# Weight splits placed behind the next copies, the first loads reordered, and one-column PSUM clears in a four-block transformer kernel

## The reference

```python
for l in range(2):                                   # first block
    h = h + 0.5 * swiglu(rmsnorm(h, g[l, 0]), ffn weights[l, 0])      # 1024 -> 2816 -> 1024
    u = rmsnorm(h, g[l, 1])
    cols = u @ w_in[l]                               # queries, keys, values of four attentions
    y_a, y_b, y_c, y_d = mla(..), window(..), nsa(..), diff(..)       # 512 channels each
    merged = sum(sigmoid(u @ w_gate[l, b]) * (y_b @ w_branch[l, b]))
    h = h + merged @ w_o[l]
    h = h + 0.5 * swiglu(rmsnorm(h, g[l, 2]), ffn weights[l, 1])
x = rmsnorm(h, final_g)
for i in range(2):                                   # second block
    x = x + 0.5 * rms_norm(swiglu(rms_norm(x, g[0])), g[1])
    m = dilated_attention(rms_norm(x, g[2])) if i == 0 else retention(rms_norm(x, g[2]))
    x = x + rms_norm(m, g[3])
    x = x + 0.5 * rms_norm(swiglu(rms_norm(x, g[4])), g[5])
```

## Time and profile before

| | |
|---|---|
| median of 3 runs | 2826.56 us (2824.9 to 2827.1) |
| profiled execution | 2825.75 us, span 2823.9 us |
| TensorE matmuls busy | 2744.4 us, 97% |
| VectorE, ScalarE busy | 1879.5 us (67%), 1387.9 us (49%) |
| chain that ended last | TensorE 86%, VectorE 7%, ScalarE 3% |
| DMA | 488.46 MB, 173 GB/s on average |

### The profile page before, as it was taken

One profiled execution on the slowest core, in us unless ns is written; L12 is line 12 of the kernel. 1 busy time (PEld: TensorE's weight loads), 2 busy tenths in 40 slices (PEclk: granted clock), 3 DMA queues, 4 the chain that ended last, 5 costly groups with the idle time before them and its releaser, 6 DMA issues.

```text
span 2823.9 us, 42094 instructions
## 1 busy us (share of the span) xinstructions
PE 2744.4 (97%) x16902; PEld 2401.5 (85%) x16902; DVE 1879.5 (67%) x2830; ACT 1387.9 (49%) x1950; POOL 104.0 (4%) x135
## 2 busy tenths in 40 slices
PE   7999999999999999999999999998999998999998
PEld 6888999788888989988878889997888888988787
DVE  5666678666776657867677666555667766755666
ACT  4554455454545445545555544444545454453544
POOL 1000000000000000001011001110000000000000
PEclk9999999999999999999999999999999999999999
DMA  6454443445445543346545545543554554434443
GB/s 245 180 197 164 152 157 135 179 160 197 173 184 187 193 168 147 135 162 229 183 179 195 186 175 172 175 154 136 196 181 167 188 183 155 176 134 172 164 178 127
DMA packets 49046, 488.46 MB, mean 173 GB/s; under 512 B 6480, under 2 KB 6576, under 8 KB 10520
## 3 DMA queue, kind: packets, MB, share of 16 engines
q1 hardware_dynamic: 43192, 470.44, 45.2%
q0 software_dynamic: 5728, 16.25, 2.1%
HBM read 485.47 MB, written 1.19 MB: 172 GB/s over the span
## 4 chain that ended last, share of the span: by engine, by line
PE 86%; DVE 7%; ACT 3%; issue 1%; DMA 1%; POOL 0%; DVEq 0%; ACTq 0%; SPq 0%; POOLq 0%
PE ps L859 67%; PE ps L919 15%; DVE ring_lo L1861 2%; ACT ring_hi L1504 1%; PE ps L875 1%; PE ps L1133 1%; DMA norm_g<-norm_gT_dram 1%; PE ps L1341 1%; DVE ring_lo L1874 1%; PE ps L1356 1%; DVE xn L1990 0%; ACT ring_hi L1555 0%; PE ps L1248 0%; DVE ring_lo L1917 0%; DMA ring<-stream_dram 0%
## 5 line engine op out<-in xcount | busy, mean ns | idle before, releaser
L859 PE MATMUL ps<-uT,ring_hi 128*128 128x512 f32 (+1 forms) x5536 | 1510.1, 344 | 9.8 <-DVE qkT L2020 8.3
L859 PE MATMUL ps<-uT,ring_lo 128*128 128x256 f32 x4176 | 1176.1, 282 | 0.0
L859 PEld LDWEIGHTS ps<-uT,ring_hi 128*128 128x128 f32 x5536 | 954.7, 190 | 144.5 <-issue 8.8
L859 PEld LDWEIGHTS ps<-uT,ring_lo 128*128 128x128 f32 x4176 | 794.4, 190 | 6.2
L1954 DVE TENSOR_TENSOR ring_lo<-ring,ring_hi 128x2048 fp32r<-128x2048 f32 x160 | 366.8, 2292 | 221.2 <-ACT ring_hi L1555 221.2
L1861 DVE TENSOR_TENSOR ring_lo<-ring,ring_hi 128x3072 fp32r<-128x3072 f32 (+1 forms) x114 | 365.3, 3205 | 181.7 <-ACT ring_hi L1504 181.4
L1504 ACT ACTIVATE ring_hi<-ring 128x3072 fp32r<-128x3072 f32 (+1 forms) x114 | 301.8, 2648 | 244.9 <-PE ps L859 224.5
L1555 ACT ACTIVATE ring_hi<-ring 128x2048 fp32r<-128x2048 f32 x167 | 317.4, 1901 | 0.0
L919 PE MATMUL ps<-ring_hi,hid_hi 128*128 128x512 f32 x704 | 276.7, 393 | 0.0
L919 PE MATMUL ps<-ring_lo,hid_hi 128*128 128x512 f32 x704 | 276.0, 392 | 0.0
L919 PE MATMUL ps<-ring_hi,hid_lo 128*128 128x512 f32 x704 | 274.0, 389 | 0.0
(11 more groups left out here) (314 smaller groups left out, 2778.1 us busy)
## 6 DMA issues: line engine op xcount, KB each, us to landing
ring<-stream_dram SPq DMA_DIRECT2D x299, 1536.0 KB, 6.3
mlaT_all<-bias_vectors POOLq DMA_DIRECT2D x32, 96.0 KB, 2.9
bias<-gains_dram POOLq DMA_DIRECT2D x5, 512.0 KB, 7.8
yR<-bias_vectors POOLq DMA_DIRECT2D x1, 2048.0 KB, 10.8
mlaT_all<-bias_vectors POOLq DMA_DIRECT2D x32, 64.0 KB, 2.9
row<-ret_const_dram POOLq DMA_DIRECT2D x1, 1280.0 KB, 5.7
h<-x_rows_dram POOLq DMA_DIRECT2D x2, 512.0 KB, 11.6
yR<-gains_dram POOLq DMA_DIRECT2D x2, 512.0 KB, 10.7
```

What stands on the lines that cost most here:

```text
L859: m = pe.matmul(out_, lhsT, rhs, start=start, stop=stop, **kw)
```

## The change

1. **Start.** SyncE issues table and picks, h, constants and gains, then slot 0's gate part, slot 0's up part, the first two thirds of slot 1, the last thirds of both, then slots 2 and 3. Slot 0's gate part is split in the middle of the first norm, its up part behind it, slot 1's two thirds behind the squares. GpSimd's parameter loads go behind its first root.
2. **Clears** write one column each.
3. **Mixer, t = 14:** `copy_diff` ahead of the gate, `low_diff` ahead of the gate's scaling.
4. **Output projection of the mixer:** the last third of its first slot is split on its own, early; k = 2 is multiplied first.
5. **Dilated attention:** the low split behind the first eight pieces goes behind the next piece's copy.
6. **Retention:** the query and key tiles lie 3, 3, 3, 3, 2, 2 in their slots, the last two of kind FFN; each low split goes behind the next tile's copy, the first rotation behind tile 7's; a head's last split goes behind the turned copies, and the swish behind the split.

```diff
@@ -72,6 +72,7 @@
 C_RET_QK, C_RET_V, C_RET_O = 6, 16, 6
+QR_FIRST = [0, 3, 6, 9, 12, 14]
@@ -85,12 +86,19 @@
              + _FFN + [WHOLE] * (3 * 8 + C_WO - 1) + [RAW] + _FFN
-             + _FFN + [WHOLE] * (C_RET_QK + C_RET_V + 4) + [RAW] * (C_RET_O - 4) + _FFN)
+             + _FFN + [WHOLE] * (C_RET_QK - 2) + [FFN] * 2 + [WHOLE] * (C_RET_V + 4) + [RAW] * (C_RET_O - 4) + _FFN)
...
+def ret_slot(t):
+    n = max(n for n in range(C_RET_QK) if QR_FIRST[n] <= t)
+    return n, t - QR_FIRST[n]
@@ -330,6 +338,11 @@
         h_in = sem("h_in")
+        gate_0_in = sem("gate_0_in")
+        up_0_in = sem("up_0_in")
+        front_1_in = sem("front_1_in")
+        gate_0_hi = sem("gate_0_hi")
+        gate_0_lo = sem("gate_0_lo")
@@ -745,9 +758,12 @@
         BACK_SLOTS = []
-        for first in [layer_slot(l) + C_FFN for l in range(DEPTH)] + [layer_slot_2(i) + C_FFN for i in range(DEPTH)]:
-            BACK_SLOTS += [first, first + 1]
+        for l in range(DEPTH):
+            BACK_SLOTS += [layer_slot(l) + C_FFN, layer_slot(l) + C_FFN + 1, mix_slot(l) + S_WO]
+        for i in range(DEPTH):
+            BACK_SLOTS += [layer_slot_2(i) + C_FFN, layer_slot_2(i) + C_FFN + 1]
@@ -795,8 +811,8 @@
             if what[0] == "qk":
-                if what[1] % T_PER_SLOT == T_PER_SLOT - 1 or what[1] == QR_T - 1:
-                    split_after(c0 + what[1] // T_PER_SLOT, take, end)
+                if what[1] + 1 in QR_FIRST + [QR_T]:
+                    split_after(c0 + ret_slot(what[1])[0], take, end)
@@ -806,12 +822,21 @@
-            load(stream[0, :, :], 0)
-            sp.wait_ge(table_masked, 1)
...
                 sp.dma_start(picks_sb[0:33, 512 * n:512 * n + 512], pick_1[:, 512 * n:512 * n + 512]).then_inc(picks_in, 16)
-            for s in range(1, NS):
+            loads = [(h[:, 0, :], x_rows[:, 0, :]), (h[:, 1, :], x_rows[:, 1, :]), (cst[:, :], consts),
+                     (norm_g[:, :, :, :], norm_gT)]
+            assert len(loads) == H_DMAS
+            for dst, src in loads:
+                sp.dma_start(dst, src).then_inc(h_in, 16)
+            sp.dma_start(ring[:, 0, 0:D], stream[0, :, 0:D]).then_inc(gate_0_in, 16)
+            sp.dma_start(ring[:, 0, D:2 * D], stream[0, :, D:2 * D]).then_inc(up_0_in, 16)
+            sp.dma_start(ring[:, 1, 0:2 * D], stream[1, :, 0:2 * D]).then_inc(front_1_in, 16)
+            for s in range(2):
+                sp.dma_start(ring[:, s, 2 * D:3 * D], stream[s, :, 2 * D:3 * D]).then_inc(weights_in[s], 16)
+            for s in range(2, NS):
@@ -891,8 +916,13 @@
                 def gate_up(c, t, i=None, first=False, end=False):
-                    split_weights(c, i)
+                    if c:
+                        split_weights(c, i)
                     for part in range(2):
+                        if c == 0 and part == 0:
+                            pe.wait_ge(gate_0_lo, 1)
+                        elif c == 0:
+                            split_weights(c)
@@ -927,7 +957,7 @@
                 for b in range(4):
-                    pe.matmul(ps[:, b, :], zero_bf[:, :], zero_bf[:, 0:1].to_broadcast([1, 512]),
+                    pe.matmul(ps[:, b, 0:1], zero_bf[:, :], zero_bf[:, 0:1],
@@ -956,7 +986,7 @@
                         if ks[0] == 5:
-                            pe.wait_ge(lo_back, 2 * l + a + 1)
+                            pe.wait_ge(lo_back, BACK_SLOTS.index(c) + 1)
@@ -1227,14 +1257,16 @@
                             lambda k: (merged_lo, K_SPLIT * l + k + 1) if k < K_SPLIT
-                            else (merged, 32 * l + branches_before(32) + 1 + k))
+                            else (merged, 32 * l + branches_before(32) + 1 + k), [2, 0, 1] + list(range(3, KD)))
...
                     c = c0 + k // 3
-                    split = SLOT_KIND[c] != RAW
-                    if split:
+                    split, back = SLOT_KIND[c] != RAW, c in BACK_SLOTS and k % 3 == 2
+                    if back:
+                        pe.wait_ge(lo_back, BACK_SLOTS.index(c) + 1)
+                    elif split:
@@ -1248,12 +1280,12 @@
                         elif split:
-                            mm(ps[:, n, :], x_hi[:, k, ts], high(c)[:, cols], k == 0, False)
+                            mm(ps[:, n, :], x_hi[:, k, ts], high(c)[:, cols], k == (2 if c in BACK_SLOTS else 0), False)
...
                             mm(ps[:, n, :], x[:, k, ts], slot(c)[:, cols], False, False)
-                    if k % 3 == 2 or k == nk - 1:
+                    if k % 3 == (1 if c in BACK_SLOTS else 2) or k == nk - 1:
@@ -1293,7 +1325,7 @@
                     if hp == 0 and n in (2, 5):
-                        pe.wait_ge(lo_back, 2 * DEPTH + n // 3 + 1)
+                        pe.wait_ge(lo_back, BACK_SLOTS.index(c) + 1)
@@ -1398,16 +1430,17 @@
-                for t in range(16):
-                    c = c0 + t // 3
+                for t in range(QR_T):
+                    n, place = ret_slot(t)
+                    c = c0 + n
...
                     if t in (2, 5):
-                        pe.wait_ge(lo_back, 2 * DEPTH + 2 + t // 3 + 1)
-                    tile_piece(pc[0], c, t % 3, KD * p if t == 0 else None)
+                        pe.wait_ge(lo_back, BACK_SLOTS.index(c) + 1)
+                    tile_piece(pc[0], c, place, KD * p if t == 0 else None)
...
                     pc[0] += 1
-                    if t % 3 == 2 or t == 15:
+                    if t + 1 in QR_FIRST + [QR_T]:
@@ -1517,8 +1550,17 @@
                     act.activation(dst, src, ACT.Copy, scale=gain[:, k:k + 1]).then_inc(uT_act_ready, 1)
+                    if p == 0 and k == 3:
+                        act.wait_ge(gate_0_in, 16)
+                        act.activation(high(0)[:, 0:D], ring[:, 0, 0:D], ACT.Copy).then_inc(gate_0_hi, 1)
+                if p == 0:
+                    act.wait_ge(up_0_in, 16)
+                    act.activation(high(0)[:, D:2 * D], ring[:, 0, D:2 * D], ACT.Copy).then_inc(hi_ready, 1)
                 act.activation(xn[:, 0, :], h[:, 0, :], ACT.Square, accum_out=h_sq[:, 0:1]).then_inc(h_squared, 1)
+                if p == 0:
+                    act.wait_ge(front_1_in, 16)
+                    act.activation(high(1)[:, 0:2 * D], ring[:, 1, 0:2 * D], ACT.Copy).then_inc(hi_ready, 1)
@@ -1527,6 +1569,8 @@
                     v, c = FT * f + g + 1, c0 + g
+                    if c < 2:
+                        act.wait_ge(weights_in[c], 16)
@@ -1566,6 +1610,12 @@
+            def take_high_unused(c):
+                act.wait_ge(weights_in[c % NS], 16 * (c // NS + 1))
+                act.activation(high(c)[:, 2 * D:], ring[:, c % NS, 2 * D:], ACT.Copy).then_inc(hi_back, 1)
@@ -1637,7 +1687,8 @@
                         copy_2(g, retention_copy)
-                        done_retention(g, take_high)
+                        if what == "qk" or n < 7:
+                            done_retention(g, take_high)
@@ -1664,9 +1715,10 @@
                     copies("row", hh)
-                    swishes(hh)
...
                         copies("turn", hh - 1)
+                    done_retention(ret_piece("row", hh, 7), take_high)
+                    swishes(hh)
@@ -1780,15 +1832,17 @@
                         copy_outputs(l, t - 2)
+                    if t == 14:
+                        copy_diff(l)
...
                         gate(l, merge_at(2 * t))
-                    if t == 14:
-                        copy_diff(l)
...
                 take_high(mix_slot(l) + S_BRANCH_2 + 1)
+                take_high_unused(mix_slot(l) + S_WO)
...
                     if k == 3:
-                        take_high(mix_slot(l) + S_WO)
+                        act.wait_ge(ring_used, emptied_before(mix_slot(l) + S_WO))
+                        take_high_late(mix_slot(l) + S_WO)
@@ -1800,8 +1854,6 @@
-            for c in range(2):
-                take_high(c)
@@ -1884,6 +1936,14 @@
                                              ALU.subtract).then_inc(uT_dve_ready, 1)
+                    if p == 0 and k == 3:
+                        dve.wait_ge(gate_0_hi, 1)
+                        dve.tensor_tensor(ring_lo[:, 0, 0:D], ring[:, 0, 0:D], high(0)[:, 0:D].bitcast(F32),
+                                          ALU.subtract).then_inc(gate_0_lo, 1)
+                if p == 0:
+                    dve.wait_ge(hi_ready, 1)
+                    dve.tensor_tensor(ring_lo[:, 0, D:2 * D], ring[:, 0, D:2 * D], high(0)[:, D:2 * D].bitcast(F32),
+                                      ALU.subtract).then_inc(lo_ready, 1)
@@ -2022,9 +2082,10 @@
                 copy_row(p, 5, True)
+                first_late = []
...
                     copy_2(PIECES_DIL + n, dilated_copy)
-                    done_dilated(n, take_low)
+                    done_dilated(n, take_low if n < 7 else first_late.append)
@@ -2059,6 +2120,8 @@
                     take_pieces(pieces[0:1])
+                    for c in first_late if s == 0 else ():
+                        take_low(c)
@@ -2078,12 +2141,21 @@
```

(52 more changed lines are left out.)

## The result

| | before | after |
|---|---|---|
| median of 4 runs | 2825.73 us | 2790.87 us (2789.35 to 2791.39) |
| profiled execution | 2825.75 us, span 2823.9 | 2790.96 us, span 2789.2 |

The ratio is 0.9881, with a 95% interval of 0.9867 to 0.9894: 1.2% faster, 34.9 us by the medians. Forecast were 2792.0 and a range of 2785 to 2805.

What follows compares the result with a forecast made beforehand. TensorE, its matmuls filling 97% of the span, was taken as the bound, so order should cut its idle time. Terms 8.5+3+2.6+4.3+12.3+3.0 = 33.7 us off 2825.75 gave 2792, range 2785 to 2805.

Steps and rivals of the forecast that it cites:

- The start: First norm and FFN: earlier loads and reordered splits gain 8.5 us, ends 4 and 10.5.
- T: Start: landing of the first norm's loads, put at 8 us; first transposes before the change start at 19.20.
- clears near 19.5: First FFN: sign that the start term holds, with the first norm's transposes near 8.
- The clears: Seven later FFNs: one-column clears save about 0.5 each, less some root waits; 3 us counted, ends 0 and 6.
- up to 2.5 more: Clears: extra gain to the sum if four clears cost 0.1, by the Trainium skill's 25 ns each.
- t = 14, the turns: Mixer step 14, both layers: earlier copies gain 2.6 us; retention's turned heads: copies first gain 3.0 us.
- The output projection: Mixer, both layers: first-slot wait goes, 0.9 returns at the second slot, layer 1's clock stays up; gain 4.3 us.
- Dilated attention and retention's tiles: Copies ahead of splits and new slot layout remove copy waits, a value-slot wait and low clock; gain 12.3 us.
- (a): Rival: new waits replace old at roots, second output slot and retention's VectorE; half the sum but the start, about 2805; chance 0.16.
- (b): Rival: start gains little, matmuls waiting for slot 0's gate part behind h; 2800 us; chance 0.13 together with (c).
- (c): Rival: retention's reorder fails because splits come late instead of copies; about 2800 us; chance 0.13 together with (b).
- (d): Rival: slower, as TensorE's granted clock is low more often behind remaining waits; 2837 us at 90 us more low; chance 0.02.

Runs made afterwards that it cites:

- e1: Changed kernel with a one-column ScalarE copy ahead of its first wait, so the table load is done before h lands: 2788.93 us, ratio 0.9874.
- e2: Changed kernel with ten unused transposes behind the first norm's sixteen, in TensorE's gap before the first FFN matmul: 2790.06 us, ratio 0.9881.
- w1: Changed kernel with the output projection's first slot split whole again, k in the order 0, 1, 2: 2795.36 us, ratio 0.9901.
- r3: Changed kernel with only retention's first rotation moved back behind tile 3, splits still behind the next copy: 2794.71 us, ratio 0.9896.
- r1: Changed kernel with retention's query and key tiles in slots of 3, 3, 3, 3, 3 and 1 again, order as changed: 2792.98 us, ratio 0.9888.
- r2: Changed kernel with VectorE's old order of splits and rotation in retention's query and key tiles, slot layout as changed: 2793.7 us, ratio 0.9894.
- f1: Changed kernel with twenty unused transposes ahead of the wait for h in each of the second block's six norms: 2785.54 us, ratio 0.9864.

## Why the prediction was right

**The start** is where a step failed. The forecast's chain from T was "ScalarE's first copy starts 1.2 after the transposes"; it starts 2.5 after them, because of a table load that in the trace of before lay in the first microseconds, under the wait for slot 0, and that the moved splits no longer pulled forward. That is an instruction of the step that was moved, and it was not counted; e1 shows it. The first FFN matmul came at T+6.3 for a forecast T+5.5, 0.8 late, because the four copies behind the load took 1.56, less than the forecast gave them. The second is "a half of gate and up is 16 matmuls and takes about 2.8": the gate half took 5.3, because the chain had opened a gap of 2.6 between transposes and matmuls and TensorE's clock stood at its lower level behind it (e2). The forecast named it ("a lower clock could stretch the first matmuls") and gave it half a microsecond; it cost 2.4. That the root would be half a microsecond late did not show: the slow matmuls hid it (GpSimd ends at 21.97, the clears begin at 23.47), and it came out only where they were made fast (e2, 0.81). GpSimd's root itself took 2.70 for 1.56 counted; why was not looked into. The landing was right to 0.8; the forecast's own terms end at 4.2 (0.8 and 3.4), and the latency that makes 8 of it had no row. The sum closes: of the 9.3 that the forecast's chain gives (11.2 less 1.9) the landing takes 0.8, the chain to the first matmul 0.8 and the slow gate half 2.5, while the root that was not late gives back 0.5 and the shorter clears 0.3, which leaves 6.0 for 5.9 measured. The sign that the forecast named for this term, clears near 19.5, did not come: they began at 23.47. At 5.9 the term lies within its ends, 4 and 10.5.

**The clears** gave 4.1 in seven for 3 forecast. The length of the short clears was mis-sized: 0.18 for four instead of 0.5, and in two FFNs part of the difference became a wait for the root, as was said. (The forecast's "up to 2.5 more" for clears of 0.1 is 2.8 by its own figures, 0.4 in each of seven.)

**t = 14, the turns**: 2.8 for 2.6, 3.5 for 3.0; in both the old wait is gone but for 0.2. The surplus at the turns is a matter of how idle time is counted: from the modelled end of the last matmul, 0.38 behind its start. Where nothing is waited for, the next matmul begins 0.03 behind that start (2456.15 after 2456.12 in the kernel after), where before it began 1.87 behind it; so a wait of 1.49 is worth 1.84 at first and 1.75 after the next few matmuls.

**The output projection**: 4.8 for 4.3. The remaining wait before the second slot was forecast at 0.9 and is 0.76. That the low clock of layer 1 would go was right here, but w1 shows that it is not layer 1's own: the dip may come in either layer.

**Dilated attention and retention's tiles**: 13.3 for 12.3, no wait left; the copy waits and the low clock behind them, as counted. r3 confirms the place of the rotation, r1 the layout's share.

**The rivals.** (a) new waits take half: one new wait of 2.6 in the start, and elsewhere only the 0.8 of each output projection that was forecast. (b) the start gains little: half true, by another cause than the gate part's landing. (c) did not occur. (d), slower through the low clock: 20.4 us at the low level ahead of the end after against 30.6 before (stretches of 3.4 and 6.8 us in each, that of the start left out), so it went the other way. The two errors, start and the rest, nearly cancel, which is luck; the total is better than its parts.

## What to carry to other kernels

An engine's in-order queue is also a priority list: put a long piece of work that is wanted late behind the short one that somebody waits for, and count what then stands in one row (r3). When a first step moves ahead, look for what used to be done in its shadow: table loads, a warm clock. And a wait of TensorE can cost more than its length, by the clock behind it; where it can't be removed, fill it with matmuls that nobody reads.

## What the runs showed of the hardware

- Behind TensorE's waits of 2.06 (r1), 2.37 (w1), 2.93 (r2), 3.84 (r3) and the norms' 3.0 the granted clock fell to its lower level for 3.4 or 6.8 us. It is not sure each time: of two waits of 2.37 in one execution of w1 only one was followed by low clock, and in the kernel after a norm's wait of 3.00 and one of 2.42 in dilated attention were not. A 3.4 us stretch costs about 1.7: w1 loses 3.2 in the layer that has one and 1.6 in the other.
- Twenty unused transposes in a wait kept the clock up at six of six norms; ten of them in the start brought the full rate from the first matmul (pairs of 0.35 instead of 0.64).
- ScalarE's table load took 1.28, and the copy behind it began 0.02 later. The Trainium skill (ScalarE: Activation LUTs, What ACT_TABLE_LOAD costs) adds a drain of 1380 ns to each switch; no row here shows one, and e1 gained no more than 1.2.
- The landing of the first loads differed from execution to execution of like kernels: in ten with the same first loads the first transposes began between 8.20 (r1) and 9.19 (f1).
